# The expert stage of a decoder trunk written out, with each next expert's token rows fetched by an indirect transfer and transposed

## The reference

```python
for layer in range(DEPTH):
    h = rms_norm(x, attn_norm_g[layer])
    proj = h @ w_in[layer]                       # q | k | v | conv value | conv gate
    ...                                          # q, k normalised per head
    attn_out = sliding_window_attention(q, k, v, sinks[layer])
    conv_out = conformer_conv(proj[..., o_c:o_g], proj[..., o_g:], conv_w[layer], ...)
    x = x + jnp.concatenate([attn_out, conv_out], axis=-1) @ w_out[layer]
    h = rms_norm(x, ffn_norm_g[layer])
    if layer % 2 == 0:
        x = x + dense_swiglu(h, dense_w_gate[i], dense_w_up[i], dense_w_down[i])
    else:
        x = x + moe_swiglu(h, w_router[i], moe_w_gate[i], moe_w_up[i], moe_w_down[i])

def moe_swiglu(h, w_router, w_gate, w_up, w_down):
    logits = (t @ w_router).astype(jnp.float32)
    top_v, top_i = lax.top_k(logits, TOP_K)      # TOP_K = 2 of N_EXPERTS = 8
    top_w = jax.nn.softmax(top_v, axis=-1)
    combine = ...                                # each token's weight for each expert
    for e in range(N_EXPERTS):                   # w_gate[e], w_up[e]: 1024 x 3584, w_down[e]: 3584 x 1024
        y = (jax.nn.silu(t @ w_gate[e]) * (t @ w_up[e])) @ w_down[e]
        out = out + combine[:, e:e + 1] * y
```

## Time and profile before

| what | value |
|---|---|
| median of 3 timed runs | 1451.32 us (1450.49 to 1452.38) |
| profiled execution, its own time | 1446.28 us |
| its span, first to last instruction | 1444.7 us |
| mean granted TensorE clock | 0.98 of full |
| PE busy | 1372.9 us (95% of the span) |
| DVE, ACT, POOL busy | 1076.3, 915.5, 53.7 us |
| moved by DMA | 428.10 MB |

### The profile page before, as it was taken

One profiled execution on the slowest core, in us unless ns is written; L12 is line 12 of the kernel. 1 busy time (PEld: TensorE's weight loads), 2 busy tenths in 40 slices (PEclk: granted clock), 3 DMA queues, 4 the chain that ended last, 5 costly groups with the idle time before them and its releaser, 6 DMA issues.

```text
span 1444.7 us, 19503 instructions
## 1 busy us (share of the span) xinstructions
PE 1372.9 (95%) x7441; PEld 1162.3 (80%) x7442; DVE 1076.3 (74%) x715; ACT 915.5 (63%) x731; POOL 53.7 (4%) x77
## 2 busy tenths in 40 slices
PE   6998999989988999999999999999999999999994
PEld 5867999979667888888788888878888888888883
DVE  5555444553656888888888898888888888888883
ACT  4564434344554777767776777767677677777771
POOL 3220000010200000000000000000000000000001
PEclk9999999989988999999999999999999999999997
DMA  9545655643624999999999999999999999999992
GB/s 323 157 138 170 202 174 181 211 145 108 206 88 145 368 342 363 393 370 336 372 378 339 376 386 340 343 392 368 339 373 392 343 372 390 358 355 382 390 343 103
DMA packets 198951, 428.10 MB, mean 296 GB/s; under 512 B 9304, under 2 KB 45392, under 8 KB 198864
## 3 DMA queue, kind: packets, MB, share of 16 engines
q1 hardware_dynamic: 195392, 416.71, 80.6%
q0 software_dynamic: 3472, 10.21, 1.9%
HBM read 415.42 MB, written 6.82 MB: 292 GB/s over the span
## 4 chain that ended last, share of the span: by engine, by line
PE 90%; DVE 4%; ACT 2%; DMA 1%; issue 1%; SPq 0%; POOL 0%; POOLq 0%; ACTq 0%; DVEq 0%
PE ps L1006 88%; DVE w_low L728 2%; PE ps L1209 2%; ACT w_high L514 1%; DMA raw<-in_w_in 1%; DMA raw<-y_slots,row_i 0%; PE ps L1029 0%; DVE hT_both L751 0%; SPq L344 0%; DVE h_td L744 0%; PE ps L1117 0%; DVE work_b L776 0%; DVE mx L769 0%; DVE h_td L833 0%; ACT sc L585 0%
## 5 line engine op out<-in xcount | busy, mean ns | idle before, releaser
L728 DVE TENSOR_TENSOR w_low<-raw,w_high 128x2048 fp32r<-128x2048 f32 x391 | 896.3, 2299 | 232.1 <-ACT w_high L514 231.6
L514 ACT ACTIVATE w_high<-raw 128x2048 fp32r<-128x2048 f32 x391 | 749.2, 1917 | 267.3 <-PE ps L1006 263.3
L1006 PE MATMUL ps<-w_high,hT_both 128*128 128x512 f32 (+1 forms) x1920 | 602.8, 391 | 13.2 <-issue 5.9
L1006 PEld LDWEIGHTS ps<-w_high,hT_both 128*128 128x128 f32 x1920 | 361.5, 189 | 86.9 <-issue 11.4
L1006 PE MATMUL ps<-w_low,hT_both 128*128 128x512 f32 (+1 forms) x960 | 372.2, 388 | 0.0
L1006 PE MATMUL ps<-w_high,act_both 128*128 128x512 f32 x1072 | 342.9, 391 | 1.8 <-DVE act_both L909 1.8
L1006 PEld LDWEIGHTS ps<-w_high,act_both 128*128 128x128 f32 x1072 | 202.2, 189 | 43.7 <-DVE act_both L909 2.1
L1006 PEld LDWEIGHTS ps<-w_low,hT_both 128*128 128x128 f32 x960 | 182.1, 190 | 35.0
L1006 PE MATMUL ps<-w_low,act_both 128*128 128x512 f32 x536 | 209.4, 391 | 0.0
L1006 PE MATMUL ps<-hT_both,w_high 128*128 128x256 f32 x960 | 177.5, 285 | 2.6 <-DVE hT_both L751 2.6
L1006 PEld LDWEIGHTS ps<-hT_both,w_high 128*128 128x128 f32 x960 | 152.1, 193 | 3.8 <-DVE hT_both L751 2.8
(11 more groups left out here) (184 smaller groups left out, 582.7 us busy)
## 6 DMA issues: line engine op xcount, KB each, us to landing
raw<-in_moe_w_gate SPq DMA_DIRECT2D x112, 1024.0 KB, 7.2
raw<-in_moe_w_up SPq DMA_DIRECT2D x112, 1024.0 KB, 7.2
raw<-in_moe_w_down SPq DMA_DIRECT2D x112, 1024.0 KB, 6.9
raw<-in_w_in SPq DMA_DIRECT2D x14, 1024.0 KB, 7.0
raw<-in_dense_w_gate SPq DMA_DIRECT2D x11, 1024.0 KB, 5.3
raw<-in_dense_w_up SPq DMA_DIRECT2D x11, 1024.0 KB, 5.4
raw<-in_dense_w_down SPq DMA_DIRECT2D x11, 1024.0 KB, 4.9
raw<-in_w_out SPq DMA_DIRECT2D x8, 1024.0 KB, 6.8
```

Source lines behind the costliest of these rows:

```text
L514: act.activation(w_part[0][:, s % PART_RING, :], raw[:, s % RAW_RING, :], ACT.Copy).then_inc(w_high_done, 1)
L728: dve.tensor_tensor(w_part[1][:, q, :], raw[:, r, :], w_part[0][:, q, :], ALU.subtract).then_inc(w_low_done, 1)
L1006: return pe.matmul(out_, lhsT, rhs, start=start, stop=stop, skip_group_check=True)
```

## The change

Three things are changed in the expert stage, and nothing in the stages ahead of it but the preparation for them.

1. The loops over pairs of experts are gone on PE, ACT, DVE and SP: `expert_steps` is called once for all eight experts, and all 56 steps are written out (PE's program grows from 2940 to 4205 rows). POOL's loop over the stores is written out too.
2. The rows of experts 1 to 7 no longer come from a matmul with `onehot`. POOL stores the normalised tokens `h_td` to DRAM (`h_rows`), and for each next expert fetches its 128 rows of 4 KB by an indirect transfer into `xrows`; at the same place in the steps as before, PE transposes them (eight transposes) into the same PSUM banks. Expert 0 still uses `gather`.
3. The indices of these fetches, `slot_tok[place, e]`, are the token numbers: PE multiplies `onehot` with a column of token numbers `tok` (16 matmuls with one moving column, into PSUM bank 7), and DVE casts them to integers. `tok` is made by POOL ahead of layer 1's convolution.

```diff
+            pool.iota(tok_i[:, :], pattern=[[P, NB]], base=0, channel_multiplier=1).then_inc(tok_ready, 1)
+            pool.wait_ge(tok_ready, 1)
+            pool.tensor_copy(tok[:, :], tok_i[:, :]).then_inc(tok_ready, 1)
             conv(1)
+            for b in range(NB):
+                pool.wait_ge(h_done, 6 + b + 1)
+                pool.dma_start(h_dram[b * P:(b + 1) * P, :], h_td[:, b, :]).then_inc(h_stored, 16)
             n_passes = passes_in_all(pool)
+            pool.wait_ge(slots_listed, 1)
+            pool.wait_ge(h_stored, 16 * NB)
+
+            def fetch(e):
+
+                pool.wait_ge(gathered, 2 * e)
+                pool.indirect_dma_start(out=xrows[:, :], out_offset=None, in_=h_dram[:, :],
+                                        in_offset=bass.IndirectOffsetOnAxis(ap=slot_tok[:, e:e + 1], axis=0)).then_inc(rows_read, 16)
...
-            with pool.Fori(0, NE) as e:
+            for e in range(NE):
+                if e + 1 < NE:
+                    fetch(e + 1)
                 store(e)
```

DVE, behind `place()` (SP and ACT have the same exchange of the loop for one call):

```diff
+            dve.wait_ge(slots_summed, 1)
+            dve.tensor_copy(slot_tok[:, :], ps[:, 7, 0:NE]).then_inc(slots_listed, 1)
             n_passes = passes_in_all(dve)
...
-            with dve.Fori(0, NE // 2 - 1) as i:
-                expert_steps(S_MOE + 4, 0, 0, 2, True, i, (PAIR, 2 * EG, 2))
-            expert_steps(S_MOE + 4 + (NE // 2 - 1) * PAIR, (NE - 2) * EG, NE - 2, 2, False, None, (0, 0, 0))
+            expert_steps(S_MOE + 4, 0, 0, NE, False, None, (0, 0, 0))
```

PE:

```diff
+            def turn_rows(i, per, e):
+
+                pe.wait_ge(rows_read, at(i, 16 * per, 16 * e))
+                for j in range(2):
+                    for k in range(4):
+                        last = pe.transpose(ps[:, (3, 6)[j], k * P:(k + 1) * P], xrows[:, (4 * j + k) * P:(4 * j + k + 1) * P], ident[:, :])
+                    last.then_inc(gathered, 1)
...
                         if k % EG == GATHER_AT and (k // EG + 1 < experts or following):
-                            gather(i, per_e, e + k // EG + 1, e_reg(k // EG + 1))
+                            turn_rows(i, per_e, e + k // EG + 1)
...
             gate_up(S_MOE, 0, None, 0)
             pe.wait_ge(onehot_done, 4)
+            pe.wait_ge(tok_ready, 2)
+            for e in range(NE):
+                for b in range(NB):
+                    last = mm(ps[:, 7, e:e + 1], onehot[:, b, e, :], tok[:, b:b + 1], e == 0 and b == 0, b == NB - 1)
+            last.then_inc(slots_summed, 1)
             n_passes = passes_in_all(pe)
             pe.wait_ge(prod_done, DG + 1)
             turn_act()
-            with pe.Fori(0, NE // 2 - 1) as i:
-                expert_steps(S_MOE + 4, 0, 0, 2, True, i, (PAIR, 2 * EG, 2), lambda k: i * 2 + k)
-            expert_steps(S_MOE + 4 + (NE // 2 - 1) * PAIR, (NE - 2) * EG, NE - 2, 2, False, None, (0, 0, 0), lambda k: NE - 2 + k)
+            expert_steps(S_MOE + 4, 0, 0, NE, False, None, (0, 0, 0))
```

More of the change, by code:

```diff
@@ L113, in hybrid_trunk @@
         iota_c = sb("iota_c", [P, P])
+        xrows = sb("xrows", [P, D])
+        tok_i = sb("tok_i", [P, NB], I32)
+        tok = sb("tok", [P, NB])
+        slot_tok = sb("slot_tok", [P, NE], I32)
         base_e = sb("base_e", [P, NE])
@@ L139, in hybrid_trunk @@
         MAX_OVER = (2 * S) // (P + 1)
+        h_dram = nc.dram_tensor("h_rows", (S, D), F32, kind="Internal").ap()
         y_dram = nc.dram_tensor("y_slots", ((NE + MAX_OVER) * P, D), F32, kind="Internal").ap()
@@ L248, in hybrid_trunk @@
         gathered = sem("gathered")
+        tok_ready = sem("tok_ready")
+        h_stored = sem("h_stored")
+        slots_summed = sem("slots_summed")
+        slots_listed = sem("slots_listed")
+        rows_read = sem("rows_read")
         xg_high_done = sem("xg_high_done")
@@ L408, in one_pass @@
                 expert_steps(S_OVER + 4, (e,), None, m, OVER)
-            with sp.Fori(0, NE // 2 - 1) as i:
-                expert_steps(S_MOE + 4, (i * 2, i * 2 + 1), (i * 2 + 2, 0), i, PAIR)
-            expert_steps(S_MOE + 4 + (NE // 2 - 1) * PAIR, (NE - 2, NE - 1), None, None, 0)
+            expert_steps(S_MOE + 4, range(NE), None, None, 0)
             overflow_passes(sp, passes_in_all(sp), one_pass)
@@ L693, in _ @@
             high(S_MOE + 5)
-            with act.Fori(0, NE // 2 - 1) as i:
-                expert_steps(S_MOE + 4, 0, 0, 2, True, i, (PAIR, 2 * EG, 2))
-            expert_steps(S_MOE + 4 + (NE // 2 - 1) * PAIR, (NE - 2) * EG, NE - 2, 2, False, None, (0, 0, 0))
+            expert_steps(S_MOE + 4, 0, 0, NE, False, None, (0, 0, 0))
             def one_pass(e, m):
@@ L1210, in turn_act, with expert_steps @@
                 last.then_inc(act_turned, 1)
-            def expert_steps(s, n, e, experts, following, i, pers, e_reg):
+            def expert_steps(s, n, e, experts, following, i, pers):
                 per_s, per_n, per_e = pers
@@ L1293, in one_pass @@
                 turn_act()
-                expert_steps(S_OVER + 4, NE * EG, NE, 1, False, m, (OVER, EG, 1), None)
+                expert_steps(S_OVER + 4, NE * EG, NE, 1, False, m, (OVER, EG, 1))
             overflow_passes(pe, n_passes, one_pass)
```

## The result

The changed kernel took 1424.14 us (median, 1423.59 to 1426.98), the kernel before beside it 1450.9: a ratio of 0.982, 95% interval 0.9803 to 0.9838, so 26.8 us less between the medians. I had forecast 1429.6 us, 21.7 less, with a range of 1424.0 to 1438.5. It ran a second time later: 1424.58 us, ratio 0.9826 (0.9811 to 0.9841). The profiled execution took 1423.88 us, its span is 1422.3; against the profiled execution of before that is 22.4 us.

A forecast was written before the change was run, and what follows sets the result against it. PE was taken to bound the expert stage; -19.0 (gathers to transposes), -6.5 (loops) and +3.8 (token numbers) gave -21.7 us, applied to the median 1451.32 us: 1429.6 us, range 1424 to 1438.5.

The forecast's parts named there:

- The bound: Expert stage: PE alone sets the time at 16.79 us a step; DMA is busy but ahead.
- Gather out, transposes in: Experts 1 to 7: seven gathers off PE, 25.1 us, eight transposes each added, 6.1 us; net -19.0 us.
- Loops out: Expert stage: writing out the loop removes PE's two jumps back, 3.2 us each; -6.5 us.
- Token numbers in: Start of expert stage: 16 one-column matmuls on PE delay DVE and the steps; +3.8 us (0 to 7.5).
- The sum: Whole kernel: -21.7 us from the profiled execution's 1446.28 us, giving 1424.6 us.
- my own bounds: Whole kernel: -25.5 us with token matmuls for nothing to -14.6 us with both uncertain PE terms bad; 1425.8 to 1436.7.
- 1 (transfers as the bound): Expert stage: queues can't exceed 370 GB/s where 381 is wanted; +2.8 us, 1454 us; chance 5%.
- 2 (ring dry now and then): Weight slots: late loads lose 1.3 us per expert, 9 us in all; -12.6, 1438.7 us; chance 12%.
- 3 (written-out code stalls): PE's longer program: late instruction fetch gives back the 6.5 us; -15.2, 1436.1 us; chance 8%.
- 4 (fetch too late): Row fetch by POOL: served so late that PE waits; within 0.2% of 1451.3 us; chance 2%.

The follow-up runs named there:

- loops-only kernel: Kernel before with all loops of the expert stage written out, POOL's too, gathers kept as matmuls, no token numbers: 1441.41 us, ratio 0.9941.
- the later cast: Changed kernel with DVE's wait for the token matmuls and its cast moved behind the first prod_t and two low parts: 1420.88 us, again 1420.6 us.

## Why the prediction was right, and where its sizes were off

**The bound.** Right: PE's steps set the time on both sides, 16.79 us each, and what PE was spared in them shows in full.

**Gather out, transposes in.** Right: -19.0 forecast, -18.8 in the trace, with eight transposes at 0.87 us as worked out. DVE's low part after them was to fit by 0.7 us; it fitted by 1.1: `gate_up` ended at 526.95, the pair of low parts began at 530.35, its first was through by 532.63, and PE went on at 533.74 without a gap. The fetches landed in 4.2 to 9.4 us; the last was issued at 1182.7 us and wanted at 1237.9.

**Loops out.** The mechanism was right, shown from both sides (PE alone gives all, the others nothing). The size was that of one execution: -6.5, where ten jumps give 8.1 on the mean and the medians of the loops-only kernel 9.3 (the six jumps of the kernel before alone: 7.4). My step that failed is "That is 2.96 + 0.26 = 3.2 us each". It took the 0.26 for a constant; it is 0.26 with the clock kept, and up to 1.9 with the clock fallen, as at five of the ten.

**Token numbers in.** 3.7 us of matmuls forecast, 3.69 measured; the start of the steps forecast at about 463.2, measured at 462.68. That the price is DVE's wait and not the matmuls was shown by the later cast. The 1.4 us of a longer first step was not in my sum. It isn't due to the token matmuls: from turn to turn the first step is 21.5 us in this trace, and 20.9 to 21.5 us in the five other traces of kernels without them (20.1 in the first profile of before).

**From the sum to the number.** The sum, 1424.6, was within 0.7 us of the profiled execution, 1423.88. That is in part luck: two terms that the sum didn't have, 1.6 us less in the last `down` and 1.4 us more in the first step, nearly cancel. I then added 5.0 us because the profiled execution of before lay that far under the median, as if it were a constant of measuring. It wasn't: the profiled execution of after stands at its median (1423.88 and 1424.14). Four executions of before that day went from 1448.9 to 1452.4, and later ones from 1443.8 to 1454.8; the profile was a short one of these. Much of this spread lies ahead of the expert stage, where the two kernels hardly differ: of the 8.6 us between the two later profiles of before, 6.3 are there before the first `turn_act`. The medians are 4.4 us further apart than the two profiles; falls at the jumps, of which the first profile had none, explain about 1.6 us of that. The last `down` was at the higher clock in both traces of the changed kernel and for half of it at the lower in two of three of before, 1.6 us each. Both happen on either side: with gathers it was long in four of six traces (7.3 to 7.4 us), with fetches in one of seven (7.35 us, a trace of the later cast). So the change doesn't decide it alone, and whether it shifts the odds so few traces can't tell. Two to three us stay open. They may be nothing: the interval of the measured difference is 23.5 to 28.6 us, and the second pair of medians is 25.7 us apart. My number, 21.7 us less, lies outside that interval, and 1424.14 us lies outside my own bounds of 1425.8 to 1436.7; the stated range held it by 0.14 us, because it had been widened at the low end for the spread of the runs.

**The rivals.** 1 (transfers as the bound): false at 381 GB/s, but the limit is near: at about 400 it came true with six more fetches. 2 (ring dry now and then): false; no wait of ACT for a load, though single loads took up to 11.8 us, more than the 8 to 10 that I had named, with a median of 7.5, less. 3 (written-out code stalls): false, no such wait of PE. 4 (fetch too late): false by more than 40 us; the last fetch had 55 us from issue to use, and none took more than 9.4.

## What to carry to other kernels

In this kernel a loop on the engine that bounds the stage cost its jumps, and more than the idle time at them where the clock fell behind it; the loops of the other engines cost nothing that the runs could show. When side work is given to an engine that idles, look at who waits for its result: the work was free here, the wait placed ahead of the next product was not, and moving one wait behind three instructions won it back. And a sum made from one profiled execution is no better than executions agree (three of before took 1443.8, 1446.3 and 1452.4 us); it needs more than one execution of before.

## What the runs showed of the hardware

Standing still for 2.9 to 3.0 us at a jump, PE lost its 2.4 GHz in some executions (18.0 to 18.2 us for the next 72 matmuls) and kept it in others (16.6 us), with the same program. In three of the five falls PE came back to the lower clock, in two the clock fell only after it had gone on, and after 3 to 4 us it was back. At the start of the stage it fell while PE was busy without a pause: in the second trace of the changed kernel the granted clock is 1.00 from 457 to 458 us, 0.81 in the next microsecond and 0.50 behind it, and PE ran token matmuls from 455.7 to 459.8 us. A fetch that POOL issued took 0.99 to 2.37 us of POOL in the stage, where the indirect transfers at the end, with DVE idle, took 0.94 to 1.02; four of the seven fetches took 0.99 to 1.02 all the same, what made three longer isn't shown, and nothing waited for them. Matmuls with one moving column and 128x128 float32 weights took 0.115 us a record (3.69 / 32), those with eight 0.149 at a granted clock of 0.77, which is 0.115 at full clock: the number of columns made no difference there. Of a gather's records with 128 columns, one took 0.112 (3.59 / 32).
